# Forget-gate sums in a fused two-block transformer kernel: from broadcast tiles added on VectorE to eight rows added inside PSUM

## The reference, cut to what matters

```
log_f = log_sigmoid(f_logit + b_forget)          # 256 tokens x 8 heads
c     = cumsum(log_f, axis=tokens)
s     = (q . k) * 64**-0.5 + c[query] - c[key]
p     = softmax(where(key <= query, s, -inf))
o     = p @ v
```

## Time and profile before

| what | value |
|---|---|
| median of 3 runs | 1838.15 us (1836.23 to 1838.55) |
| the profiled execution | 1835.39 us |
| its span in the trace | 1833.6 us |
| PE busy | 95% of the span |
| DVE busy | 83% |
| ACT busy | 66% |
| DMA, from the first expert on | about 428 GB/s |
| granted TensorE clock, mean | 0.991 |
| fox attention | from 760.2 us |
| expert loop, first matmul | about 887 us |

### The profile page before, as it was taken

The page is one execution under the profiler, slowest core; times in us unless marked ns, Lnnn a source line. Parts: engine busy times, 40 slices in busy tenths (PEclk is TensorE's granted clock), DMA queues, the critical chain, the costliest instruction groups (busy, mean ns, idle before and its releaser), DMA issues.

```text
span 1833.6 us, 26401 instructions
## 1 busy us (share of the span) xinstructions
PE 1747.9 (95%) x10404; PEld 1524.0 (83%) x10404; DVE 1520.7 (83%) x1285; ACT 1218.6 (66%) x949; POOL 134.9 (7%) x140
## 2 busy tenths in 40 slices
PE   8999999999999999999999999999999999999996
PEld 7977899989899989988877877778777787777775
DVE  5787556578556666678899999999999999999997
ACT  5465444433333345545788988889898898888985
POOL 1255000000000001431000000000000000000000
PEclk9999999999999999999999999999999999999999
DMA  7521345554345455327699999999999999999994
GB/s 284 191 92 70 138 178 200 206 207 144 132 175 195 180 215 198 104 88 280 276 428 427 429 427 429 427 429 429 428 428 429 428 429 429 428 429 428 428 428 179
DMA packets 40646, 544.13 MB, mean 297 GB/s; under 512 B 4625, under 2 KB 4753, under 8 KB 5905
## 3 DMA queue, kind: packets, MB, share of 16 engines
q1 hardware_dynamic: 40592, 543.39, 72.2%
HBM read 542.33 MB, written 1.05 MB: 296 GB/s over the span
## 4 chain that ended last, share of the span: by engine, by line
PE 61%; DMA 12%; ACT 6%; issue 6%; DVE 4%; POOL 1%; DVEq 0%; ACTq 0%; POOLq 0%; SPq 0%
PE psum L1411 19%; PE psum L987 12%; DMA ring<-in_w 12%; PE psum L837 7%; PE psum L997 6%; PE psum L1425 4%; ACT arena_r L1822 4%; PE psum L1440 2%; DVE ring_r L2338 2%; PE psum L880 2%; PE psum L1176 1%; PE psum L897 1%; PE psum L1349 1%; PE psum L1313 1%; PE psum L1473 1%
## 5 line engine op out<-in xcount | busy, mean ns | idle before, releaser
L2338 DVE TENSOR_TENSOR ring_r<-ring,arena_r 128x4096 fp32r<-128x4096 f32 x192 | 846.4, 4418 | 16.0 <-ACT arena_r L1822 12.1
L1822 ACT ACTIVATE arena_r<-ring 128x4096 fp32r<-128x4096 f32 x188 | 682.3, 3629 | 62.4 <-DMA ring<-in_w 61.9
L1411 PE MATMUL psum<-arena_r,stream_r 128*128 128x512 f32 x1024 | 410.9, 401 | 11.3 <-DVE stream_r L2427 9.3
L1411 PE MATMUL psum<-ring_r,stream_r 128*128 128x512 f32 x1024 | 403.4, 394 | 0.0
L1411 PEld LDWEIGHTS psum<-arena_r,stream_r 128*128 128x128 f32 x1024 | 195.1, 191 | 56.3 <-DVE ring_r L2338 11.4
L1609 ACT ACTIVATE arena_r<-ring 128x3072 fp32r<-128x3072 f32 x40 | 110.9, 2773 | 188.9 <-DMA ring<-in_ffn 188.9
L1411 PEld LDWEIGHTS psum<-ring_r,stream_r 128*128 128x128 f32 x1024 | 194.9, 190 | 39.1
L987 PE MATMUL psum<-arena_r 128*128 128x256 f32 x672 | 190.2, 283 | 0.0
L987 PE MATMUL psum<-stream_r,ring_r 128*128 128x256 f32 x672 | 190.2, 283 | 0.0
L987 PE MATMUL psum<-stream_r,arena_r 128*128 128x256 f32 x672 | 190.1, 283 | 0.0
L1440 PE MATMUL psum<-arena_r 128*128 128x512 f32 x512 | 161.1, 396 | 11.6 <-DVE arena_r L2486 10.7
(11 more groups left out here) (336 smaller groups left out, 2687.3 us busy)
## 6 DMA issues: line engine op xcount, KB each, us to landing
ring<-in_w SPq DMA_DIRECT2D x192, 2048.0 KB, 12.8
ring<-in_ffn SPq DMA_DIRECT2D x44, 1536.0 KB, 6.4
ring<-in_w_in SPq DMA_DIRECT2D x8, 2048.0 KB, 8.2
ring<-in_in_w SPq DMA_DIRECT2D x7, 2048.0 KB, 12.7
ring<-in_out_w SPq DMA_DIRECT2D x7, 2048.0 KB, 8.2
ring<-in_l_in SPq DMA_DIRECT2D x8, 1536.0 KB, 8.3
ring<-in_proj SPq DMA_DIRECT2D x2, 2048.0 KB, 8.7
ring<-in_misc SPq DMA_DIRECT2D x1, 1632.0 KB, 9.0
```

Source lines behind the costliest of these rows:

```text
L1411: last = mm(dst, xg[:, k, :], b[:, k * D_EXPERT:(k + 1) * D_EXPERT], start=(k == 0 and b is u_hi), stop=(k == KD - 1 and b is u_lo))
L1822: A(w_hi[u % HI_SLOTS], ring[:, MOE_SLOT[at], :], ACT.Copy).then_inc(m_hi, 1)
L2338: V.tensor_tensor(ring_r[MOE_SLOT[u % NM]][:, :], raw, w_hi[u % HI_SLOTS].bitcast(F32), ALU.subtract).then_inc(m_lo, 1)
```

## The change

The running sums are made once, as eight rows (one for each head, 256 keys), already multiplied by 8, the square root of 64, since L1973 multiplies the sum by 64**-0.5. `fox_c` now has `log_f` as the stationary operand (8 columns) and `tri`/`ones` as the moving one; DVE writes the 8x256 result to `forgotten`. `forget_sums`, the PSUM tiles `fox_b0` to `fox_b5` and the DVE instructions of L1964 are gone. In the logits of fox each head's product of 64 rows is left open in PSUM and closed by a second product of eight rows: a column of the identity (rows 0 to 7, column h, broadcast to 128) picks row h of `forgotten`. The term c[query] is no longer added; the softmax over the keys of one query does not depend on it. PE waits for the drain of `fox_c` ahead of the wait for `skT`. DVE drains `fox_c` at the same place of its list as before.

```diff
 (planning)
-                    if kind == "fox":
-                        O.add(f"fox_b{u}", "dve")
                     O.add(f"{kind}_l{u}", "dve")
 (PE, logits)
                         last = mm(bank(name)[:, i * w:(i + 1) * w], q[a:a + DH, h // 2, tc * P:(tc + 1) * P],
-                                  k_of(h)[a:a + DH, 0:w], start=True, stop=True)
+                                  k_of(h)[a:a + DH, 0:w], start=True, stop=(kind != "fox"))
+                        if kind == "fox":
+                            last = mm(bank(name)[:, i * w:(i + 1) * w], ident[0:8, h:h + 1].to_broadcast([8, P]),
+                                      forgotten[:, 0:w], start=False, stop=True)
 (PE, steps of attention)
-                        if items[t][0] == "fox":
-                            forget_sums(items[t][1])
                         logits(*items[t])
 (PE, ahead of attention)
-            mm(bank("fox_c")[:, 0:8], tri, log_f[:, 0, :], start=True, stop=True)
-            mm(bank("fox_c")[:, 8:16], ones, log_f[:, 0, :], start=True, stop=False)
-            end("fox_c", mm(bank("fox_c")[:, 8:16], tri, log_f[:, 1, :], start=False, stop=True))
+            mm(bank("fox_c")[0:8, 0:P], log_f[:, 0, :], tri, start=True, stop=True)
+            mm(bank("fox_c")[0:8, P:T], log_f[:, 0, :], ones, start=True, stop=False)
+            end("fox_c", mm(bank("fox_c")[0:8, P:T], log_f[:, 1, :], tri, start=False, stop=True))
 ...
+            pe.wait_ge(*O.drained("fox_c"))
             pe.wait_ge(*O.drained("skT"))
 (DVE, masked)
-                    if kind == "fox":
-                        name = f"fox_b{u}"
-                        dve.wait_ge(*O.ready(name))
-                        for i, h in enumerate(heads):
-                            last = V.scalar_tensor_tensor(fox_d[:, u % 2, i * w:(i + 1) * w], bank(name)[:, i * w:(i + 1) * w],
-                                                          fox_c[:, tc, h:h + 1], mask_of[kind](tc), ALU.subtract, ALU.add)
-                        drain(name, last)
-                        mask = fox_d[:, u % 2, :].rearrange("p (a b) -> p a b", a=nh)
-                    else:
-                        mask = mask_of[kind](tc).unsqueeze(1).to_broadcast([P, nh, w])
+                    mask = mask_of[kind](tc).unsqueeze(1).to_broadcast([P, nh, w])
 (DVE, after split("gs1"))
             dve.wait_ge(*O.ready("fox_c"))
-            drain("fox_c", V.tensor_copy(fox_c[:, :, :], bank("fox_c")[:, 0:16].rearrange("p (a b) -> p a b", a=NT)))
+            drain("fox_c", V.tensor_scalar(forgotten, bank("fox_c")[0:8, 0:T], DH ** 0.5, None, ALU.mult))
```

More of the change, by code:

```diff
@@ L362, in program @@
         arena_at[0] = shared - 4 * T
-        sqT, skT, sv, fox_d = carve(4, T), carve(2, T), carve(NT, P), carve(2, 512)
+        sqT, skT, sv, forgotten = carve(4, T), carve(2, T), carve(NT, P), carve(2, 512)[0:8, 0, 0:T]
         HIGH_OUT2 = [STREAM, 1024]
@@ L373, in program @@
         stat_at[0] = 240
-        f_in, log_f, fox_c, f_neg, f_u, f_tmp = few(NT, 8), few(NT, 8), few(NT, 8), few(NT * 8), few(NT * 8), few(5, NT * 8)
+        f_in, log_f, f_neg, f_u, f_tmp = few(NT, 8), few(NT, 8), few(NT * 8), few(NT * 8), few(5, NT * 8)
         pos_f, rope_k = few(NT), few(NT, 32)
@@ L902, in out_rows @@
                         last.then_inc(part_used, 1)
-            def forget_sums(u):
-                tc, _, heads, wd = UNITS[u]
-                name = f"fox_b{u}"
-                begin(name)
-                for i, h in enumerate(heads):
[L910 to L916, removed]
             OPERANDS = {
```

## The result

The changed kernel takes 1854.59 us (median of 6 runs, 1852.2 to 1857.79) against 1838.16 us (6 runs, 1836.23 to 1839.6): ratio 1.0091, interval 1.0079 to 1.0103, that is 16.4 us slower. The sign was forecast; the size was not, and the time lies 6 us above the range. The profiled execution took 1853.98 us, its span is 1852.2 us.

A forecast was written before the change was run, and what follows sets the result against it. PE was taken to bound the time up to the expert loop, the weight stream and DVE within it. Wait 2.4 + records and shape changes 2.9 + clock 1.5 = 6.8 us, giving 1845.0 us; range 1838.2 to 1848.5.

The forecast's parts named there:

- The sign: Whole kernel: slower, with a chance of 0.58, against 0.38 for within 0.2% and 0.04 for faster.
- What ties PE to the end: SP's queue: expert loads start at PE's release at 891.27 us, so each microsecond PE loses earlier moves the end equally.
- rival 2: Expert stage: the loss is absorbed later because DVE and DMA bound the loop; about 0 to +1, 1838.7 us; chance 0.13.
- The new wait: Ahead of the first fox logits: PE waits for DVE's drain of fox_c, +2.4 us (2.1 to 2.6).
- The changes of shape: Fox units: each alternation between 64-row and eight-row products costs 0.21 us (0 to 0.33).
- The sum of changes and removed records: Fox units 0 to 5: added shape changes less saved records, +2.9 us (-2.0 to +5.2).
- rival 1: Fox units: eight-row and 64-row products alternate without a gap; +1.9 us, 1840.1 us; chance 0.20.
- rival 3: Fox units: products in different rows overlap, so removed blocks come off whole; -4.1 us, 1834.1 us; chance 0.05.
- The clock: Behind the wait ahead of attention: one stretch at half clock after about 3.1 us idle, +1.5 us (0 to 3.0).
- if eight rows stream like 128: Fox units: assumed eight-row records take 128-row time, saving 0.45 us in each of units 2 to 5.

The follow-up runs named there:

- kernel 6: Changed kernel with the small products on 128 rows (120 of zeros), alternating, and fox_c drained ahead of gs1: 1839.16 us, ratio 1.0008.
- kernel 3: Changed kernel with each unit's products grouped, first the logits and then the eight-row products, new wait kept: 1852.49 us, ratio 1.0085.
- kernel 1: Kernel before the change with only PE's wait for the drain of fox_c added: 1840.41 us, ratio 1.0016.
- kernel 4: Changed kernel with the small products on all 128 rows, 120 of them zeros, wait and alternation kept: 1843.86 us, ratio 1.0036.
- kernel 2: Changed kernel with DVE's drain of fox_c moved ahead of its low half of gs1, products unchanged: 1851.63 us, ratio 1.0087.
- 5: Changed kernel with fox_c drained ahead of gs1 and each unit's products grouped, still eight rows: 1844.97 us, ratio 1.0038.
- 7: Changed kernel with small products on 128 rows (120 of zeros), grouped in each unit, and fox_c drained ahead of gs1: 1834.71 us, ratio 0.9983.
- kernel 8: Changed kernel with small products on 64 rows, in the same array half as their logits, alternating, fox_c drained early: 1842.11 us, ratio 1.0014.

## Why the prediction was wrong in size

- **What ties PE to the end** (the stream starts when PE gives back the first expert weights): right. A delay of 17.7 us at SP's queue came out as 18.6 us in the profiled executions, and rival 2, which had it absorbed, fell.
- **The new wait**, forecast 2.4 us (2.1 to 2.6): 2.1 us more idle time, at the lower bound, with the drain at 0.40 us where 0.42 was taken. Right. PE began its logits at 761.21 and not at 762.56, since DVE came to its low half 1.4 us earlier in this execution.
- **The changes of shape**, forecast 0.21 us each and 3.4 to 3.6 us for unit 1: 0.19 us and 3.31 us. The sum of changes and removed records, forecast +2.9, is +1.8 us in kernel 6 (by the medians, with the interval given there), where nothing else is left. Slightly too dear; rival 1 (alternation is free) fell, since grouping the products of kernel 6 gives 1839.16 - 1834.71 = 4.5 us back. The rule on changing the tiling mode that the prediction cites from the Trainium skill, TensorEngine Tiling (Array Packing), Key Properties, agrees with these rows.
- **The overlap of products** in different rows (rival 3): nothing of it. No pair starts before the one ahead of it has streamed, in unit 1 as in unit 0. The rows of kernel 3 say the same of products that stand in groups.
- **The clock**, forecast +1.5 us (0 to 3.0): this is the step that failed. It took the low clock to be a matter of a long idle stretch ahead of it, since the two low stretches in the earlier trace rows both followed one of 3 us, and so counted one short stretch. For that one stretch the term was roughly of the right size: it is 6.8 us long in kernel 1, where wait and clock together are 3 to 4 us, and 10.2 us long in the changed kernel, where kernel 4 less kernel 6, less 2.1 for the wait, makes it about 3 us. What was missing is that the change replaces products of 128 rows by products of eight, and that PE's clock falls under those although PE is busy the whole time. Of the 16.4 us, 2.1 are the wait, 1.8 the alternation less the removed records, and by subtraction about 12.5 are left for the clock, where 1.5 was the term: about 3 for the stretch behind the wait and 9 to 10 for the later ones. That fits the 10 us that kernel 4 gets back. The 37.5 us at half clock can cost up to 18.8; some of it lies where PE waited for POOL before, of which the stage now has nothing.

The rows for the effect of the rows addressed were in the trace only from one side: in the stage before, 128-row sums stood between the 64-row logits of every unit, and the clock never fell. The prediction counted the columns of both kinds as equal, which they are for the time at a given clock ("if eight rows stream like 128": they do, kernel 3), and asked no further. But the same trace did show that an idle stretch of 3 us isn't needed. It has four more low stretches, all in the expert loop, from 1195.8, 1311.9, 1547.4 and 1680.5 us on. Each begins behind a wait of only 0.9 to 1.5 us for ACT, among or just behind 16 records of 64 columns. The first of them, in the timeline and the windows of the kernel before:

```profile
1193.52 1.10 PE L1425 MATMUL psum<-small,arena 128*128 128x64 f32 x8 [1.50 <-ACT arena L1838]
```

```profile
1195.90:1199.20 3.30, 3.30 (x9) 2.62 (x8) 2.84 (x2) 2.25 (x2) 0.00 (x0) 0.50 0.98 417
```

Shown is that the later low stretches go with the rows addressed. Three pairs of kernels differ in them alone, and in each the one with eight rows is about 10 us slower or more: the changed kernel against 4 (ratios 1.0091 and 1.0036), 2 against 6 (1.0087 and 1.0008), 5 against 7 (1.0038 and 0.9983). What the added rows carry doesn't matter, since 120 rows of zeros serve (4). Neither the long idle stretch (2) nor the alternation (3) nor either of the two (5) is needed for the low clock, but they aren't without weight. Taken away alone each gives back about 3 us or less, and together (5) 9 to 10 us, where the wait measured 2.1 and the alternation 4.5. How the three act together on the clock is not shown. No run separates the rows from the shape of the array that goes with them. Not settled either is how many rows are enough between 64, where it seems to go either way, and 128; nor why the low stretches differ in length.

## What to carry to other kernels

A matmul with few rows takes the same columns as a full one and saves nothing by itself; if it replaces full ones in a busy stretch, look at the granted clock there, and try padding it to all rows with zeros if the clock falls. Group the products of one shape, and put the small drain that releases PE ahead of a long piece of work on DVE. A kernel that loses more than the sum of its waits and records is to be read window by window for its clock. And where a forecast takes the low clock from one kind of place, look at every low stretch that the trace has, and at what PE did ahead of each.

## What was not expected of the hardware

- PE was busy for 10.00 of 10.00 us and had a granted clock of 0.50, that is 1.2 GHz, from 788.3 us for 23.9 us, with no idle stretch ahead of it after 761.21 us; with the small product on 128 rows, zeros included, it stayed at 1.00, that is 2.4 GHz, through the stage (kernel 6). The Trainium skill, TensorE: Matmul & The Clock Gate, Part 1, describes a monitor that sets the clock by how busy PE has been, and warns of long idle gaps and of frequent short ones. By that rule alone kernel 2, which has no gap in the stage that kernel 6 hasn't, would have kept its clock as kernel 6 did, and the windows show that it didn't.
- A change of shape costs more at half clock, though less than double: a pair of 256 columns starts every 1.15 us with changes (the changed kernel) and every 0.86 without (kernel 8), 0.29 us; at full clock every 0.63 and 0.43, 0.20 us.
- Products of 8, 64 and 128 rows stream at the same rate: four of 256 columns take 1.12, 1.13 and 1.13 us at full clock (kernels 3 and 7).
